# Eight gate blocks of a token mixer as seven quadrant products for eight, with sums of weights formed by adding transfers

## What is computed

```python
proj = h @ w_in                                     # h: 512 x 1024
(r_q, r_k, r_v, r_g, m_q, m_k, m_v, m_o, m_i, m_f, gate_r, gate_m) = split(proj)
ret = head_rms_norm(retention_chunkwise(rotary(r_q), rotary(r_k), r_v)) * ret_gn_w * silu(r_g)
y_ret = ret @ w_ret_branch
hm = head_rms_norm(mlstm_chunkwise(mq, mk, m_v, i_pre, f_pre) * sigmoid(m_o)) * mlstm_gn_w
y_m = hm @ w_mlstm_branch
x = x + (sigmoid(gate_r) * y_ret + sigmoid(gate_m) * y_m) @ w_out
x = x + moe(rms_norm(x))      # per token 2 of 32 experts: (silu(t @ w_gate) * (t @ w_up)) @ w_down
out = rms_norm(x)
```

## Time and profile before

| | us |
|---|---|
| median of 3 runs | 1042.69 (1042.02 to 1044.81) |
| span of the profiled execution | 1040.3 |
| TensorE busy | 1016.0 |
| VectorE busy | 428.2 |
| ScalarE busy | 276.7 |
| GpSimd busy | 71.4 |

### The profile page before, as it was taken

The page is one execution under the profiler, slowest core; times in us unless marked ns, Lnnn a source line. Parts: engine busy times, 40 slices in busy tenths (PEclk is TensorE's granted clock), DMA queues, the critical chain, the costliest instruction groups (busy, mean ns, idle before and its releaser), DMA issues.

```text
span 1040.3 us, 12422 instructions
## 1 busy us (share of the span) xinstructions
PE 1016.0 (98%) x4701; PEld 649.2 (62%) x4701; DVE 428.2 (41%) x744; ACT 276.7 (27%) x472; POOL 71.4 (7%) x101
## 2 busy tenths in 40 slices
PE   8999999999999999999999999999999999999896
PEld 7888888888888888888886433333333333333333
DVE  5265356434533324544625223333333333333235
ACT  6343555333333334622313110000000000000012
POOL 0683000000000000000000100000000000000000
PEclk9999999999999999999999999999999999999999
DMA  9224222222222223224789799999999999999993
GB/s 326 81 82 151 64 72 80 81 81 81 82 81 82 81 81 115 89 87 163 292 323 405 302 421 420 421 420 420 421 420 420 420 420 421 420 421 421 420 415 147
DMA packets 60400, 263.97 MB, mean 254 GB/s; under 512 B 9328, under 2 KB 9520, under 8 KB 35640
## 3 DMA queue, kind: packets, MB, share of 16 engines
q1 hardware_dynamic: 57464, 257.32, 62.6%
q0 software_dynamic: 2624, 5.78, 1.5%
q10 hardware_dynamic: 256, 0.10, 0.0%
HBM read 263.17 MB, written 4.20 MB: 257 GB/s over the span
## 4 chain that ended last, share of the span: by engine, by line
PE 74%; SPq 18%; DMA 3%; DVE 2%; issue 1%; ACT 1%; DVEq 0%
PE pj L492 46%; SPq L393 13%; PE pj L712 11%; PE pj L738 6%; SPq L390 5%; DMA raw_moe<-in_w_up_dram 3%; PE cb L449 3%; PE cb L748 2%; PE cb L749 1%; DMA raw_mix<-in_w_in_dram 1%; PE cb L512 1%; PE cb L541 1%; DVE sg L1555 1%; PE cb L545 1%; PE cb L548 0%
## 5 line engine op out<-in xcount | busy, mean ns | idle before, releaser
L712 PE MATMUL pj<-raw_moe,xT 128*64 128x512 f32 x1016 | 227.6, 595 | 4.4 <-DMA raw_moe<-in_w_up_dram 2.6
L1184 DVE TENSOR_TENSOR wl<-raw_mix,wh 128x1024 fp32r<-128x1024 f32 x88 | 110.5, 1257 | 186.5 <-ACT wh L893 186.4
L712 PEld LDWEIGHTS pj<-raw_moe,xT 128*64 128x64 f32 x1016 | 72.1, 137 | 141.0 <-issue 141.0
L492 PE MATMUL pj<-wh,hTh 128*128 128x512 f32 x320 | 127.3, 398 | 0.8 <-DVE hTl L1215 0.8
L893 ACT ACTIVATE wh<-raw_mix 128x1024 fp32r<-128x1024 f32 x88 | 93.0, 1059 | 129.8 <-PE pj L492 124.0
L492 PE MATMUL pj<-wl,hTh 128*128 128x512 f32 x320 | 124.9, 390 | 0.0
L492 PE MATMUL pj<-wh,hTl 128*128 128x512 f32 x320 | 124.6, 389 | 0.0
L738 PE MATMUL pj<-raw_moe,hf 128*64 128x512 f32 x512 | 116.7, 598 | 1.6 <-ACT hf L1129 1.6
L1537 DVE TENSOR_TENSOR x<-x,cb 128x512 f32<-128x512 f32 x120 | 76.9, 683 | 98.9 <-PE cb L749 98.9
L492 PE MATMUL pj<-hTh,wh 128*128 128x512 f32 x192 | 76.8, 400 | 0.0
L738 PEld LDWEIGHTS pj<-raw_moe,hf 128*64 128x64 f32 x512 | 34.6, 136 | 67.1 <-issue 67.0
(11 more groups left out here) (296 smaller groups left out, 1235.6 us busy)
## 6 DMA issues: line engine op xcount, KB each, us to landing
raw_moe<-in_w_gate_dram SPq DMA_DIRECT2D x64, 1024.0 KB, 26.8
raw_moe<-in_w_down_dram SPq DMA_DIRECT2D x64, 1024.0 KB, 26.7
raw_moe<-in_w_up_dram SPq DMA_DIRECT2D x63, 1024.0 KB, 26.1
raw_mix<-in_w_in_dram SPq DMA_DIRECT2D x32, 1024.0 KB, 5.1
raw_mix<-in_w_ret_branch_dram SPq DMA_DIRECT2D x4, 1024.0 KB, 5.0
raw_mix<-in_w_mlstm_branch_dram SPq DMA_DIRECT2D x4, 1024.0 KB, 5.9
raw_mix<-in_w_out_dram SPq DMA_DIRECT2D x4, 1024.0 KB, 5.0
xt<-in_x_dram SPq DMA_DIRECT2D x4, 512.0 KB, 6.6
```

The costliest lines, as they stand in the source:

```text
L492: m = nc.tensor.matmul(pj[:, i, :], lhsT, rhs, start=k == 0 and n == 0, stop=k == KD - 1 and n == 2)
L712: mm = nc.tensor.matmul(pj[a * CAP:(a + 1) * CAP, up, :], xT[:, 4 * half + k, a * CAP:(a + 1) * CAP], weights_of(m + a)[:, k, :], start=ha ...
L1184: V.tensor_tensor(wl[:, q % RING, :, :], raw_mix[n % MIX_RAW][:, 2 * (q % 2):2 * (q % 2) + 2, :], wh[:, q % RING, :, :].bitcast(F32), ALU. ...
```

## The change

Each of the four gate products is cut into quadrants: tokens into lower and upper 256 (i), rows of weights into lower and upper 512 (k), columns into two blocks of 512 (c). Seven products of 256 tokens x 512 rows x 512 columns take the place of the eight of the plain way (`U_11, U_21, U_T1, U_22, U_T2, U_T3, U_T4`). Three of them (U_11, U_21, U_22) read plain quadrants of weights, and the four others read sums of two to four quadrants. The sums of activations (`first21`, `second`, `fourth`, and a third that overwrites a quadrant of `hTh` and `hTl`) are formed once, by GpSimd, with head and tail by ScalarE and VectorE. The sums of weights are formed anew for each gate: GpSimd issues a DMA that adds a quadrant from DRAM to what lies in the place, in two parts of 512 KB (`weight_sum`, n = 0 to 3), so 32 such transfers beside the 16 plain loads of a quadrant. There are now four places `raw_mix`. A gate needs 14 heads and 14 tails of 128 x 1024, two for each product, where its two blocks had 8 of each.

A product has two halves s (one bank each, 128 tokens or 256 columns), 12 matmuls of 512 columns, or 24 of 256 columns where channels are on the partitions (`gate_r`, `gate_m`). U_11, T2, T3 and T4 accumulate in banks 0 and 1, the others in banks 2 and 3, and between the products the running content of a bank is copied out or added: ScalarE empties after U_11, T1, T2 and T4 (`fast_evict`), VectorE adds or subtracts after U_21, T2 and T3 (`upper_left`, `upper_right`, `lower_right`). The Sigmoids then run from SBUF (`gate_sigmoid`), except for T4's. The mLSTM's 16 steps stand after the halves in `ATTENTION`; the gating of the retention moves to GpSimd (`ret_gated`), its scaling to ScalarE (`ret_scaled`); four of the first eight turns stand in the last gate, four in block 16. The expert part is not changed.

```diff
+FAST = (B_RG, B_GR, B_GM, B_MO)
+U_11, U_21, U_T1, U_22, U_T2, U_T3, U_T4 = range(7)
+TURNS = {(3, 4, 1): (0,), (3, 5, 0): (1,), (3, 5, 1): (2,), (3, 6, 0): (3,), (B_WR, 0): (4, 5), (B_WR, 1): (6, 7),
+         (B_WR, 3): (8, 9), (B_WR + 1, 0): (10, 11), (B_WR + 1, 1): (12, 13), (B_WR + 1, 2): (14, 15)}
+ATTENTION = [1 + (26 * i + 7) // 15 for i in range(16)]
...
+        raw_mix = [at(f"raw_mix{s}", k, [P, 4, 512]) for s, k in enumerate((144.0625, 152.0625, 160.0625, 56))]
...
+            def quadrants(p):
+                if p == 0:
+                    sp.wait_ge(r_o, 12)
+                else:
+                    sp.wait_ge(wl_ok, fast_entry(p - 1, U_22, 1) + 1)
+                quadrant(p, U_11, 0, 0)
...
+            def product_half(p, u, s):
...
+                for v in range(2):
+                    q = fast_entry(p, u, v)
+                    if s == 0:
+                        pe.wait_ge(wl_ok, q + 1)
+                    for kk in range(2):
+                        k = 2 * v + kk
+                        for c in range(2 if columns else 1):
...
+                            for n, (lhsT, rhs) in enumerate(ops):
+                                m = nc.tensor.matmul(o, lhsT, rhs, start=u in (U_11, U_21, U_T1) and k == 0 and c == 0 and n == 0,
+                                                     stop=k == 3 and n == 2, skip_group_check=True)
...
+            for p in range(len(FAST)):
+                for u in range(PRODUCTS):
+                    for s in range(2):
+                        x = 2 * (PRODUCTS * p + u) + s
+                        product_half(p, u, s)
+                        if x == 0:
+                            ml_scores(0)
+                        if x in ATTENTION:
+                            i = ATTENTION.index(x)
+                            ml_products(*divmod(i, 4))
+                            if i < 15:
+                                ml_scores(i + 1)
...
             def mix_head(q):
-                n = q // 2
-                act.wait_ge(raw_in[n % MIX_RAW], 16 * (n // MIX_RAW + 1))
+                act.wait_ge(*entry_ready(q))
                 if q >= RING:
-                    wait_mix_pair(act, q - RING)
+                    act.wait_ge(*entry_used(q - RING))
...
+            def fast_half(p, u, s):
+                x = 2 * (PRODUCTS * p + u) + s
+                before = half_before(x)
+                if x and before[1] != U_11:
+                    fast_evict(*before)
...
+                mix_head(fast_entry(p, u, s) + LEAD)
+                if after >= 0:
+                    ml_output(after)
+                if before[1] == U_11:
+                    fast_evict(*before)
+                if u == U_T1:
+                    gate_sigmoid(p, 0, 0, s)
...
+            def weight_sum(p, n, v):
+                if n == 0:
+                    pool.wait_ge(wl_ok, fast_entry(p, U_11, v) + 1)
+                if n == 1:
+                    pool.wait_ge(wl_ok, fast_entry(p, U_T1, v) + 1)
+                if n == 2:
+                    pool.wait_ge(*fast_landed(p, U_T3))
+                if n == 3:
+                    pool.wait_ge(wl_ok, fast_entry(p, U_T2, v) + 1)
...
+                pool.dma_start(raw_mix[slot][:, 2 * v:2 * v + 2, :],
+                               w_in[0][512 * k + 256 * v:512 * k + 256 * (v + 1), c0:c0 + 512].rearrange("(k p) n -> p k n", p=P),
+                               accum_op=ALU.add).then_inc(sum_in[v], 16)
...
+            def ret_gated(i, j, s):
...
+                own(G.tensor_tensor(h, h, (sgq if (i, j) == (1, 0) else sgt)[:, s, :], ALU.mult))
+                out_ = rvo[:, 2 * i + s, 512 * j:512 * (j + 1)]
+                G.tensor_tensor(out_, out_, h, ALU.mult).then_inc(ret_ok, 1)
...
+            weight_sums(0, 2)
+            for s in range(2):
+                ret_gated(0, 0, s)
+            weight_sums(0, 3)
...
+            for s in range(2):
+                weight_sum(1, 0, s)
+                ret_gated(1, 0, s)
```

More of the change, by code:

```diff
@@ L641, in turn_stream @@
+            for b in range(B_WR, BLOCKS):
+                block_of(b)
             def turn_stream(t):
-                pe.wait_ge(free[t], BLOCKS)
+                pe.wait_ge(free[t], free_of(t, BLOCKS - 1))
                 for half in range(2):
@@ L1092, in square @@
+            for b in range(B_WR, BLOCKS):
+                evict_block(b - 1)
+                block_of(b)
+            evict_block(BLOCKS - 1)
             def square(t):
-                act.wait_ge(free[t], BLOCKS)
+                act.wait_ge(free[t], free_of(t, BLOCKS - 1))
                 if t >= 1:
@@ L1357, in _, with ml_normed, block_of @@
                     merged_tail(ct)
-                if b == BLOCKS:
-                    break
+            def ml_normed(half, n):
+                dve.wait_ge(sq_ok, TT * (n + 2))
+                rstd(3 + n, ssq[:, 8 * half:8 * half + 8], 8, DV)
+                for t in range(TT):
+                    for a in range(2):
+                        hv = mva[:, t, 2 * half + a, 0:DV]
+                        m = V.tensor_scalar(hv, hv, stat[:, 2, 4 * a + t:4 * a + t + 1], None, ALU.mult)
+                m.then_inc(hm_ok, 1)
+            def block_of(b):
                 if b == B_WM + 1:
@@ L1439, in _ @@
[L1439 to L1455 removed]
+                        if j == 2:
+                            part_tail(0)
@@ L1456, in _, with upper_left @@
+                    for n in TURNS.get((b, j), ()):
+                        out_tail(n)
+                    if b == B_WR and j in (0, 2):
+                        ml_normed((1, 0)[j // 2], j // 2)
                 if b == B_RV:
                     rq_turned(3)
+            def upper_left(p, s):
+                dve.wait_ge(free[s], B_RG + 4 * p + U_11 + 1)
+                dve.wait_ge(full[2 + s], full_fast(p, U_21, s))
+                h = home(p, 0, 0, s)
+                V.tensor_tensor(h, bank_view(p, 2 + s), h, ALU.add).then_inc(free[2 + s], 1)
@@ L1460, in _ @@
+            for s in range(2):
+                ml_gated(1, 0, s)
+            for b in range(B_WR, BLOCKS):
+                evict_block(b - 1)
+                block_of(b)
+            evict_block(BLOCKS - 1)
             for t in range(TT):
@@ L1689, in _, with combined @@
             pool.dma_start(gbc[:, :, :], g_dram.to_broadcast([P, H, T])).then_inc(gb_in, 16)
+            G = nc.gpsimd
+            lower, upper = slice(0, 256), slice(256, 512)
+            low, high = slice(0, 4), slice(4, KD)
+            def combined(dst, first, terms):
+                for n, (term, op) in enumerate(terms):
+                    m = G.tensor_tensor(dst[:, :, :], (dst if n else first)[:, :, :], term.bitcast(F32), op)
+                    if n < len(terms) - 1:
+                        own(m)
+                m.then_inc(rope_ok, 1)
@@ new lines, in _ @@
+            weight_sums(0, 0)
+            pool.wait_ge(mqk_ok, 8)
+            combined(thirdf, hTh[:, low, lower].bitcast(F32),
+                     ((hTh[:, low, upper], ALU.subtract), (hTl[:, low, lower], ALU.add), (hTl[:, low, upper], ALU.subtract)))
+            weight_sums(0, 1)
+            weight_sums(0, 2)
+            for s in range(2):
+                ret_gated(0, 0, s)
+            weight_sums(0, 3)
+            for s in range(2):
+                ret_gated(0, 1, s)
+            for s in range(2):
+                ret_gated(1, 1, s)
```

565 lines of the change are left out of this document (403 added, 162 removed).

## The result

The changed kernel takes 1109.41 us (median of 4 runs, 1108.42 to 1112.3) where the kernel before takes 1042.76: a ratio of 1.0641 (95% interval 1.0624 to 1.0659), 66.7 us slower. The forecast was 1027.7, from 1018 to 1045. The profiled execution has a span of 1106.6 us.

What follows compares the result with a forecast made beforehand. TensorE was taken to bound the mixer, where the gates lie, and the weight stream the experts. Matmuls -17.8 us plus stalls 2.8 gave -15.0: span 1025.3, median 1027.7 us, range 1018 to 1045.

Steps and rivals of the forecast that it cites:

- Regimes, and the saving passed on one for one: Whole kernel: TensorE sets the mixer, the weight stream the experts; what the gates save arrives at the end.
- Rival D: Expert stream: it ends when it ends, so the saving doesn't arrive; 1042.7 us, chance 0.06.
- Term 1: Gate matmuls on TensorE: 256-column ones cost 120 ns each, 17.8 us saved in all.
- Rival B: 256-column matmuls in the gates: 190 ns each because loads don't overlap; slower, 1074.7 us, chance 0.08.
- Term 2: Heads, tails and evictions on ScalarE and VectorE: hidden beside matmuls except 1 us stalls at two first-gate places.
- term 3: Adding transfers of weight sums: 5 us each, TensorE waits only beyond some 12 us; 0.8 us stall from GpSimd's order.
- rival A: First two gates: the other engines become the bound; 11.2 us of stall for 2.8, 1036.1 us, chance 0.15.
- Rival C: Adding transfers: 15.6 us each, three times a plain one, costing 43 us; slower, 1070.9 us, chance 0.09.
- The sign that I had set for this term: Gate weight sums: the 32 adding transfers land in 3 to 8 us; over 12 would speak for Rival C.

Runs made afterwards that it cites:

- e5: e1_ring2 with GpSimd's third combination held until VectorE's root is done and T4's first-gate transfers issued ahead of the gated retention pieces; 1031.72 us, ratio 0.9900.
- e1_ring2: Changed kernel with 2048 instead of 1024 bytes per partition for descriptors of GpSimd's transfers, small scratch tiles moved; 1044.15 us, ratio 1.0015 to the kernel before.
- e7: e1_ring2 with only one wait added: GpSimd starts the third combination after VectorE's root for the retention's norms; 1041.57 us, ratio 0.9987.
- e2_plain: Changed kernel with the addition left out of the 32 transfers, still 1024 bytes; 1524.52 us, not comparable since gate values differ; first expert chunk at 495.2 us.

## Why the prediction was wrong

*Regimes, and the saving passed on one for one: right.* The first expert chunk moved by +66.0 us and the time by +66.7 in the changed kernel; by -11.2 and -10.8 in e5. Rival D is refuted, in both directions.

*Term 1: right.* 120 ns taken, 120 measured. Rival B is refuted. The Trainium skill's rule that loads overlap only across groups of rows (TensorE: Matmul & The Clock Gate, Part 3, The mechanism) doesn't hold for these matmuls: matmuls of 256 columns follow each other every 120 ns, each with its own full-height load, and a load alone is shown with 190.

*Term 2: too small for the change as it was written.* I had 2.0 us here, 2.8 with the 0.8 of GpSimd's order in term 3. With the queue out of the way the stretch holds 13.8 us of waits (e1_ring2) and about 4 us of low clock, so even without the failure of term 3 the time would have been 1044.15 and not 1027.7. Two causes made most of it, and I had neither: VectorE's root shut out by GpSimd, and T4's first transfers behind the gating. This is near rival A, whose price was 11.2 us, though A had it in all gates. Only with both mended (e5) is it 4.8 us, and the clock stays full; -17.8 + 4.8 is -13.0, and -11.2 came (the other 1.8 us are not traced). I had put a late sum behind `ret_gated` between the first and second gate at 0.8 us; the same thing inside the first gate cost some 8. On the first, I had quoted the Trainium skill (SBUF — State Buffer, Who interferes with whom), which says that a VectorE instruction with two SBUF inputs and a GpSimd one that reads SBUF block each other outright, and set against it a mean that lengthened by a tenth. By that rule the root's operations with two inputs would wait out an addition, and e1_ring2 and e7 agree for two of them: 1.88 us for 0.17 (L1486) and 2.21 for 0.17 (L1488). The longest, 3.66 us for 0.23 (L1478), reads a single tile, so that sentence of the page does not cover it. A mean over long tails hides what happens to a short instruction in a chain.

*Term 3: here it failed.* "TensorE waits once a transfer takes longer than some 12 us from its issue", with 5 us for a transfer. The 5 us was near (5.8), and the slack was there. But I reckoned each transfer by itself, from its issue to its landing, and never asked how often one can be issued. The bound I gave the term was a latency; what decided was a rate, one per 6.1 us, eight per gate, 48.6 us where gate follows gate in 42.7 with the larger room. I checked the rate only as bytes (220 GB/s, "there is room"). Rival C had the right engine, the right number of links and even the sentence that the next transfer must wait for the one before to land, but hung it on a landing of 15.6 us and "decides from 13.3": it read 5.8 as safe, where by its rate, as an estimate, the term turns at 42.7 / 8 = 5.3 us from issue to issue. The forecast's own 5 us, eight times over, is 40 us, already the length of a gate (38.3 to 40.3 us of matmuls). The sign that I had set for this term, landings of 3 to 8 us, came true while the term failed. A transfer's landing time must be held against the gap between transfers as well as against its own slack.

The loss then grew by the clock, for which the forecast had no term: beside the 59.3 us of idle time, in pieces, about 20 us went to matmuls at a lower granted clock (24.5 by difference).

## What to carry to other kernels

Cost a queue twice: by the latency of one transfer against its slack, and by the spacing of issues against the period, for the transfers that are independent too; where an issue on GpSimd comes only when the last transfer has landed, look at the room for descriptors before anything else. A kernel tuned with few transfers on GpSimd's queue may have that room cut to the least, as here to 1024 bytes, and one added use makes it the bound. Before work is given to GpSimd, look at which short VectorE instructions in a chain stand beside it, not at the mean of the long ones.

## What the runs showed of the hardware

- Adding transfers of 512 KB with 1024 bytes per partition for descriptors: one per 6.1 us; with 2048, the two of a pair 1.5 to 4.2 us apart in the third and fourth gate, held by tails or by the sum before. Plain ones of that size go 1.6 to 2.6 us apart in 1024. The Trainium skill says that the rings of GpSimd's transfers lie in a part of SBUF kept for them (DMA: Bandwidth & Descriptors, SWDGE vs HWDGE vs iDMA); that its size can be the bound is what these runs add.
- An addition costs the DMA engines about twice a plain load. On GpSimd's queue the same 16.78 MB took 35.3% of 300 us with the addition and 17.9% without it (rows above, e2_plain): 6.3 us of all 16 engines per MB, and 3.2. With the room for it this was hidden: DMA share up to 1.0 in e5's windows, and no wait of TensorE is put down to it.
- GpSimd additions of 128x1024 stretch VectorE's 128x16 operations from 0.2 to as much as 3.7 us, and a 128x1024 tail from 1.22 to 3.4.
